# Rotary embedding of the first block on GpSimd, chunk by chunk, and one transpose group per weight tile

## The reference

```python
def diff_attention(h, w_qkv, w_o, lq1, lk1, lq2, lk2, subln_g, lam_init, cos, sin):
    qkv = h @ w_qkv                                    # 256x1024 @ 1024x3072
    q, k, v = jnp.split(qkv, 3, axis=-1)
    q = q.reshape(B_, S, A_N_HEADS, 2, A_HEAD_DIM)     # 8 heads, 2 halves of 64
    k = k.reshape(B_, S, A_N_HEADS, 2, A_HEAD_DIM)
    q = jnp.concatenate([apply_rope(q[..., :A_ROT], cos, sin), q[..., A_ROT:]], axis=-1)   # A_ROT = 16
    k = jnp.concatenate([apply_rope(k[..., :A_ROT], cos, sin), k[..., A_ROT:]], axis=-1)
    lam = (jnp.exp(jnp.sum(lq1 * lk1)) - jnp.exp(jnp.sum(lq2 * lk2)) + lam_init)
    ...                                                # softmax of q k^T, p0 - lam * p1, times v
```

## Time and profile before

| | us |
|---|---|
| median of 3 runs | 1056.72 |
| lowest, highest | 1055.93, 1057.69 |
| the profiled execution | 1057.23 |
| its span on the core | 1055.5 |
| its mean granted TensorE clock | 0.989 of full |

### The profile page before, as it was taken

The page is one execution under the profiler, slowest core; times in us unless marked ns, Lnnn a source line. Parts: engine busy times, 40 slices in busy tenths (PEclk is TensorE's granted clock), DMA queues, the critical chain, the costliest instruction groups (busy, mean ns, idle before and its releaser), DMA issues.

```text
span 1055.5 us, 12741 instructions
## 1 busy us (share of the span) xinstructions
PE 1001.1 (95%) x4744; PEld 820.3 (78%) x4744; DVE 735.9 (70%) x1030; ACT 543.0 (51%) x882; POOL 59.3 (6%) x100
## 2 busy tenths in 40 slices
PE   3899879999999999999999999999999999999997
PEld 2787567888888877777888887888889878888786
DVE  5989777977768787887765545737654676767753
ACT  3354654644434376665444435665555475555441
POOL 2100021000000410010000001100000010000000
PEclk9999889999999999999999999999999999999999
DMA  9999313998889845248875553856544357665551
GB/s 339 315 370 350 102 61 106 352 342 274 266 299 328 299 160 200 75 125 257 292 227 185 177 197 101 266 170 199 145 134 149 111 183 236 180 182 180 177 179 41
DMA packets 126966, 219.86 MB, mean 208 GB/s; under 512 B 9235, under 2 KB 78088, under 8 KB 126904
## 3 DMA queue, kind: packets, MB, share of 16 engines
q1 hardware_dynamic: 125488, 216.05, 62.3%
q0 software_dynamic: 1088, 2.87, 1.0%
q10 hardware_dynamic: 328, 0.12, 0.0%
HBM read 217.96 MB, written 1.05 MB: 207 GB/s over the span
## 4 chain that ended last, share of the span: by engine, by line
PE 80%; DVE 10%; ACT 4%; DMA 3%; issue 2%; POOL 0%; SPq 0%; DVEq 0%; POOLq 0%; ACTq 0%
PE bank L1815 15%; PE bank L1817 15%; PE bank L1816 15%; PE bank L1830 5%; PE bank L1831 5%; PE bank L1832 5%; DVE w_lo L1100 3%; PE bank L1877 2%; PE bank L1879 2%; PE bank L1878 2%; ACT w_hi L620 1%; DMA raw<-in_a_w_qkv 1%; PE bank L1933 1%; PE bank L1860 1%; PE bank L1909 1%
## 5 line engine op out<-in xcount | busy, mean ns | idle before, releaser
L1100 DVE TENSOR_TENSOR w_lo<-raw,w_hi 128x1024 fp32r<-128x1024 f32 x312 | 378.3, 1223 | 229.2 <-ACT w_hi L620 228.9
L620 ACT ACTIVATE w_hi<-raw 128x1024 fp32r<-128x1024 f32 x312 | 326.3, 1059 | 344.8 <-PE bank L1817 189.0
L1815 PE MATMUL bank<-w_hi,h_hi 128*128 128x512 f32 x768 | 307.4, 400 | 4.6 <-DVE h_lo L1281 2.7
L1817 PE MATMUL bank<-w_hi,h_lo 128*128 128x512 f32 x768 | 300.7, 392 | 0.0
L1816 PE MATMUL bank<-w_lo,h_hi 128*128 128x512 f32 x768 | 300.1, 391 | 0.0
L1815 PEld LDWEIGHTS bank<-w_hi,h_hi 128*128 128x128 f32 x768 | 145.0, 189 | 35.1 <-issue 4.0
L1817 PEld LDWEIGHTS bank<-w_hi,h_lo 128*128 128x128 f32 x768 | 144.8, 189 | 31.1
L1816 PEld LDWEIGHTS bank<-w_lo,h_hi 128*128 128x128 f32 x768 | 145.2, 189 | 29.7 <-issue 1.0
L1830 PE MATMUL bank<-w_hi,u_hi 128*128 128x512 f32 x200 | 78.6, 393 | 0.8 <-ACT av L1047 0.8
L1832 PE MATMUL bank<-w_hi,u_lo 128*128 128x512 f32 x200 | 77.9, 389 | 0.0
L1831 PE MATMUL bank<-w_lo,u_hi 128*128 128x512 f32 x200 | 77.9, 389 | 0.0
(11 more groups left out here) (317 smaller groups left out, 1258.8 us busy)
## 6 DMA issues: line engine op xcount, KB each, us to landing
raw<-in_f_w_in SPq DMA_DIRECT2D x176, 256.0 KB
ada<-in_ada_w SPq DMA_DIRECT2D x86, 512.0 KB, 5.8
raw<-in_w_in SPq DMA_DIRECT2D x46, 512.0 KB
raw<-in_f_w_out SPq DMA_DIRECT2D x44, 512.0 KB
raw<-in_w_up SPq DMA_DIRECT2D x88, 256.0 KB
raw<-in_a_w_qkv SPq DMA_DIRECT2D x24, 512.0 KB
raw<-in_w_down SPq DMA_DIRECT2D x22, 512.0 KB
raw<-in_b_w_qkv SPq DMA_DIRECT2D x12, 512.0 KB
```

The source lines that it names most:

```text
L620: nc.scalar.activation(w_hi[:, m % SPL], raw[:, m % RAW], ACT.Copy).then_inc(hi_done, 1)
L1100: ve.tensor_tensor(w_lo[:, m % SPL], raw[:, m % RAW], w_hi[:, m % SPL].bitcast(F32), ALU.subtract).then_inc(lo_done, 1)
L1815: mm(o, hi, w_hi[:, s, k], start=(u == 0 and k == 0), stop=False)
L1817: last = mm(o, lo, w_hi[:, s, k], start=False, stop=(u == 3 and k == 1))
```

## The change

Four edits, all in the first block:

1. The rotation leaves DVE. GpSimd does it chunk by chunk (chunks 0 to 3), each as soon as ACT has copied that chunk, with four instructions for a chunk: two products with the sine half of the table into `rope_t`, one product in place with the cosine half, one sum. Each covers both token tiles. A semaphore `rope_c` counts the chunks.
2. The transposes move from two groups before each of tiles 19 to 22 to one group before each of tiles 13 to 20, in the order 0 to 7. Group n waits for `rope_c` to reach n // 2 + 1; group 0 also waits for `evac` to reach 3. The copies to `qkT` follow on DVE (even groups) and ACT (odd groups).
3. Lambda on DVE is split: the two dot products at m = 7, the three small steps at m = 11.
4. The later waits on `rope_ok` count one less, since the first rotation no longer raises it.

```diff
-QK_STEPS_A = (19, 20, 21, 22)
-QK_ORDER_A = (0, 4, 1, 5, 2, 6, 3, 7)
+QK_STEPS_A = {13 + n: n for n in range(8)}
...
+            pool.wait_ge(side_in, 16 * SIDE)
+            for c in range(4):
+                pool.wait_ge(evac, c + 1)
+                q = proj[:, :, c * CH:(c + 1) * CH].rearrange("p t (h d) -> p t h d", d=64)[:, :, :, 0:16]
+                tmp = rope_t[:, :, 8 * c:8 * c + 8]
+                spread = lambda tab, n: tab.unsqueeze(2).to_broadcast([P, T, 8, n])
+                for h in range(2):
+                    last = nc.gpsimd.tensor_tensor(tmp[:, :, :, 8 * h:8 * h + 8], q[:, :, :, 8 - 8 * h:16 - 8 * h],
+                                                   spread(rope_a_sb[:, :, 1, 8 * h:8 * h + 8], 8), ALU.mult)
+                last.then_inc(rope_p, 1)
+                pool.wait_ge(rope_p, 2 * c + 1)
+                nc.gpsimd.tensor_tensor(q, q, spread(rope_a_sb[:, :, 0], 16), ALU.mult).then_inc(rope_p, 1)
+                pool.wait_ge(rope_p, 2 * c + 2)
+                nc.gpsimd.tensor_tensor(q, q, tmp, ALU.add).then_inc(rope_c, 1)
...
             for m in range(24):
-                if m in QK_STEPS_A:
-                    n = 2 * (m - QK_STEPS_A[0]) + 1
-                    f = QK_ORDER_A[n]
+                if m in QK_STEPS_A and QK_STEPS_A[m] % 2:
+                    n = QK_STEPS_A[m]
                     act.wait_ge(qk_t, n + 1)
...
+            def minus_lambda_end():
                 v_.wait_ge(setup, 4)
...
             for m in range(16):
+                if m in QK_STEPS_A and QK_STEPS_A[m] % 2 == 0:
+                    n = QK_STEPS_A[m]
+                    v_.wait_ge(qk_t, n + 1)
+                    ve.tensor_copy(qkT[:, 2 * n:2 * n + 2], bank[4 + n % 4][:].rearrange("p (k s) -> p k s", k=2)).then_inc(qk_d, 1)
                 low(QKV_A + SPL + m)
-                if m == 10:
+                if m == 7:
                     minus_lambda()
+                if m == 11:
+                    minus_lambda_end()
...
             for m in range(16, 24):
-                if m == 16:
-                    rotate(0, 32, rope_a_sb, rope_t, 4)
...
             for m in range(8, 24):
                 if m in QK_STEPS_A:
-                    pe.wait_ge(rope_ok, 1)
-                    for n in (2 * (m - QK_STEPS_A[0]), 2 * (m - QK_STEPS_A[0]) + 1):
-                        qk_transposes(n, QK_ORDER_A[n])
+                    n = QK_STEPS_A[m]
+                    if n == 0:
+                        pe.wait_ge(evac, 3)
+                    pe.wait_ge(rope_c, n // 2 + 1)
+                    qk_transposes(n, n)
```

More of the change, by code:

```diff
@@ L285, in program @@
         rope_ok = sem("rope_ok")
+        rope_p, rope_c = sem("rope_p"), sem("rope_c")
         qk_t = sem("qk_t")
@@ L767, in _ @@
             for m in range(24):
-                if m in QK_STEPS_A:
-                    n = 2 * (m - QK_STEPS_A[0]) + 1
-                    f = QK_ORDER_A[n]
+                if m in QK_STEPS_A and QK_STEPS_A[m] % 2:
+                    n = QK_STEPS_A[m]
                     act.wait_ge(qk_t, n + 1)
-                    nc.scalar.activation(qkT[:, 2 * f:2 * f + 2], bank[4 + n % 4][:].rearrange("p (k s) -> p k s", k=2),
+                    nc.scalar.activation(qkT[:, 2 * n:2 * n + 2], bank[4 + n % 4][:].rearrange("p (k s) -> p k s", k=2),
                                          ACT.Copy).then_inc(qk_a, 1)
@@ L1371, in _ @@
             for m in range(16, 24):
-                if m == 16:
-                    rotate(0, 32, rope_a_sb, rope_t, 4)
-                if m in QK_STEPS_A:
-                    n = 2 * (m - QK_STEPS_A[0])
-                    f = QK_ORDER_A[n]
+                if m in QK_STEPS_A and QK_STEPS_A[m] % 2 == 0:
+                    n = QK_STEPS_A[m]
                     v_.wait_ge(qk_t, n + 1)
-                    ve.tensor_copy(qkT[:, 2 * f:2 * f + 2], bank[4 + n % 4][:].rearrange("p (k s) -> p k s", k=2)).then_inc(qk_d, 1)
+                    ve.tensor_copy(qkT[:, 2 * n:2 * n + 2], bank[4 + n % 4][:].rearrange("p (k s) -> p k s", k=2)).then_inc(qk_d, 1)
                 low(QKV_A + SPL + m)
@@ L2097, in keys_b @@
             def keys_b():
-                pe.wait_ge(rope_ok, 2)
+                pe.wait_ge(rope_ok, 1)
                 pair_transposes_b(proj[:, :, 1024:1280], 4)
             def queries_b(p):
-                pe.wait_ge(rope_ok, 2 + p + 1)
+                pe.wait_ge(rope_ok, 1 + p + 1)
                 if p >= 2:
@@ L2275, in _ @@
                 if m == QK_STEPS[0]:
-                    pe.wait_ge(rope_ok, 7)
+                    pe.wait_ge(rope_ok, 6)
                     pe.wait_ge(gm_y, 1)
```

## The result

| | before | after |
|---|---|---|
| median, run in turn on one chip (19 runs each) | 1057.58 | 1059.24 |
| the same on a second chip (22 and 8 runs) | 1057.52 | 1059.70 |
| time of the profiled execution | 1057.23 | 1058.57 |
| its span | 1055.5 | 1056.8 |

The ratio of after to before is 1.0016 [1.0009, 1.0023] in the first series and 1.0023 [1.0013, 1.0032] in the second. So the change costs 1.7 us (1.0 to 2.4) and 2.4 us (1.4 to 3.4): slower than the forecast of +0.9, and around the border of 0.2% that was set between no change and slower. The absolute 1059.24 lies inside the range on record (1054.8 to 1060.0). Of its distance to the predicted 1057.6, 0.9 us is the kernel before itself, which ran at 1057.58 here and not at 1056.72.

The account below looks back on a forecast made before the run. PE, busy 95% of the span, was taken as the bound. Tiles 29.92, wait 3.38, transposes 3.59 and low clock 1.55 sum to 38.44 us against 37.55: +0.9, so 1057.6, range 1054.8 to 1060.0.

Parts of the forecast that it names:

- The rotation's wait goes, the one for chunk 2 comes: PE's 2.41 us loss before the old transposes goes; a 3.38 us wait for ACT's chunk 2 copy comes before tile 13.
- Lambda's split makes the wait shorter: Dot products at m = 7 spare ACT's exponential its wait for DVE, making PE's new wait 1.5 us shorter.
- The exponential right behind the table load: On ACT before the copy of chunk 2, the exponential starts 0.01 us after the table load ends.
- rival (d): On ACT, a longer wait behind the table load, making the kernel slower; chance 5%.
- The transposes cost the same in eight blocks: On PE, eight blocks of four cost 3.59 us against 3.63 for the old four blocks of eight.
- GpSimd is hidden, DVE's freed time is worth nothing: GpSimd's chunks take 2.7 to 7.9 us, hidden, counted as zero; PE is not short of `w_lo`, so DVE's time gains nothing.
- Rival (e): GpSimd is late beside busy DVE, costing once chunks exceed about 8.5 us; at 10 us +9, 1066; chance 5%.
- The low clock behind the new wait: PE's clock falls after idling 3.2 us before the first transposes, costing 1.55 us (0 to 3.2).
- Rival (b): The clock stays up behind PE's new wait: 1.55 us less, -0.7, 1056.0; chance 8%.
- Rival (a): Chunk 2 is free when PE asks: 4.0 us gained, 1052.7; half the way -2.3, 1054.4; together 9%.
- The low clock in tile 19: 4.40 - 2.72 - 0.09 = 1.59: In the kernel before, PE loses 1.59 us to low clock behind the rotation wait; counted as going with it.
- Rival (c): The clock pays twice, behind the new wait or in the attention: +2.5 us, 1059.2; chance 12%.

Follow-up runs that it names:

- lam10: The changed kernel with lambda's dot products back at m = 10 instead of m = 7; ratio to the kernel before 1.0058.
- dve15: Against steps15, the rotation of each chunk is done by DVE instead of GpSimd; ratio to the kernel before 0.9968.
- before_again: The kernel before, unedited, profiled a second time; start of tile 6 to end of tile 23 took 56.13 us, against 57.23 in its first profile.
- steps15: The changed kernel with the transpose groups before tiles 15 to 22 instead of 13 to 20; median 1054.4, ratio to the kernel before 0.9968.
- fill: The changed kernel with five unused matmuls of 128x512 in front of PE's wait for chunk 2; ratio to the kernel before 0.9998.

## Why the prediction was right in its mechanism and short in its size

The measured median of after lies in the range on record, and each link of the chain happened. The change itself came out at nearly twice the forecast or more, for one term in the main, the second to last below.

- **The rotation's wait goes, the one for chunk 2 comes.** Right. 3.02 us lost against 3.38 forecast, released by ACT's copy. It came out 0.36 shorter because PE was later relative to tile 16's transfer: tile 12's last matmul starts 0.35 after the split in after (71.58, 71.23), and 0.01 before it in before. In the other two profiles of after the idle time was 3.0, nearer to the forecast's 3.2. That the window of the first profile is 38.44 us, exactly the sum forecast, is partly luck: the wait is 0.36 too long in the sum, and the blocks of transposes and the low clock together are as much too short.
- **Lambda's split makes the wait shorter.** Right in kind; the credit of 1.5 us was too small: lam10 shows 3.6. It didn't enter the sum, because the sum took the split as done.
- **The exponential right behind the table load.** Right: 0.01 us (72.31 + 1.28 = 73.59, 73.60), now at the very place, and 0.01 or 0.02 in every other profile in which it didn't wait for DVE. So nothing but the load's 1.28 us itself stands there, and rival (d), a longer wait behind the load, falls. No run shows the case to which the forecast gave 5%, and half of that in the chance of slower.
- **The transposes cost the same in eight blocks.** Right. Tile 14 with its block takes 82.87 - 79.67 = 3.20 us against 2.72 + 0.44 = 3.16 forecast: 0.04 too little, 0.3 over the seven tiles behind later blocks.
- **GpSimd is hidden, DVE's freed time is worth nothing.** Right. Chunks took 4.4, 6.1, 5.1 and 3.6 us, inside the bounds of 2.7 and 7.9 though mostly far above the lower one. (In the lower one the 0.3 us for a chunk's waits was an estimate of mine; GpSimd's gaps between its instructions add up to 0.16 us in chunk 1 and in chunk 3. The upper bound would not quite have been hidden: four chunks of 7.9 us behind 62.2 end at 93.8, and the fourth was wanted at 93.5; so the price starts at 7.8 us a chunk and not at 8.5.) In after PE never waits for GpSimd, and dve15 shows the engine to be indifferent. Rival (e) falls.
- **The low clock behind the new wait.** Right: tile 13 lasts 4.43, 1.62 too long, against 1.55 forecast, and the clock fell in all three profiles. Rival (b) falls. One of the two cases that spoke against it, the first weight tile, was misread, though: there PE was slow before the idle time already (see the last section). Rival (a), chunk 2 free in time, happened in no profile of after. It needed the copy 3.2 us earlier, and the split of tile 16 stood 19.06, 19.21 and 19.22 us behind the start of tile 6 in the three, 19.42 in the profile before the prediction.
- **"The low clock in tile 19: 4.40 - 2.72 - 0.09 = 1.59", as a fixed term of before.** This is the mis-sized term. The 4.40 is the time of tile 19, 89.24 to 93.64, and the lower level was a granted clock of 0.50 there (89.37 to 92.37). It is there in one of four profiles. Where it is missing, the stretch is 1.13 us shorter (56.10 and not 57.23), since 0.46 is lost again, most of it by the wait for the copy to `qkT`, which the sum did not have. Over the four profiles before's stretch is 56.38 on the mean, 0.85 less than in the one profile, and the change costs 1.8 us by the profiles and not 0.9. The prediction took from the change a saving of 1.59 ("that term goes, and the 2.41 and 1.59 behind it with it") that before usually doesn't have to give. The single profile could not show this. It could have warned: in the same profile PE was idle for 1.97 us before tile 6 and its clock stayed at full (1.00 from 50.00 to 52.00), so idle time alone might not settle the outcome at 2.25.
- **Rival (c), 1059.2, has nearly the measured time, by a mechanism that did not happen.** It wanted a second low stretch in after, behind the new wait or in the attention. Behind the wait there is one, also behind 2.99, 3.02 and 6.56 us. The attention was not slower: 43.5, 44.5 and 44.7 us in after, 44.7, 44.4, 42.4 and 44.3 in before. The second "payment" was before's, missing. That the measured time comes near this rival is chance.

How often before's clock falls over many executions can't be said from four profiles. Nor is it known whether the chips differ in it, and so why the change cost 1.7 us on one chip and 2.4 on the other; the two intervals overlap (1.0 to 2.4, 1.4 to 3.4), so there may be nothing to explain.

## What to carry to other kernels

When work is moved earlier on the engine that is the bound, look up what its new place has to wait for before counting the old wait as won: here the inputs were early enough, but the PSUM bank was not, and two tiles (2 x 2.72 = 5.4 us) of delay turned +1.7 into -3.4 us. An idle time of PE is priced with the clock behind it, and where such a stretch stands in the profile before, take a second and a third profile before booking it as a saving. Test separately which of the parts pays: here the switch of engine, the larger edit, was worth nothing once the steps were right.

## What the runs showed of the hardware

- **The clock's reaction to idle time of PE is not the same in each execution.** In the projection the granted clock stayed at full behind 0.94, 1.62 and 1.96 or 1.97 us in every profile that has such a gap; behind 2.21 to 2.34 it fell in one of four; behind 2.86 to 6.56 in four of four. Over the 4.9 us from the first transposes the mean is 0.65 in before's first profile and in the three of after, 0.66 in lam10, and about 1.6 us are lost: transposes and tile together take 5.27 us in before's first profile against 3.69 in before_again, and 4.84 in each profile of after and 4.80 in lam10 against the 3.20 of tile 14 with its block.
- **PE ran at about half its pace in places where the granted clock reads 1.00** (0.43 us from one start to the next against 0.23). The prediction's second example of a fall, the first weight tile behind 2.68 us of idle time, is such a place. In before's profile its matmuls start 0.43 us apart, as in tile 19, but the row of the stretch has 1.00 where tile 19 has 0.65:

```profile
28.80 0.63 PE L1816 MATMUL bank<-w_lo,h_hi 128*128 128x512 f32 x1
29.22 0.63 PE L1817 MATMUL bank<-w_hi,h_lo 128*128 128x512 f32 x1
```

```profile
28.20:30.00 1.80, 1.79 (x4) 1.49 (x5) 1.80 (x3) 1.80 (x3) 0.00 (x0) 1.00 1.05 388
```

  And it is no fall behind the idle time of 2.68 us: PE was as slow before it. In the same profile eight transposes took 1.97 us, against 1.03 in the projection (at 93.64), and sixteen matmuls of one column 3.57 us, against 1.84 for the same shape in before_again. The clock column reads 1.00 for them too:

```profile
19.37 1.97 PE L1922 MATMUL bank<-ident,xn 128*128 128x128 f32 x8 [3.42 <-DVE xn L1146]
...
21.95 3.57 PE L1933 MATMUL bank<-ones,ada_acc 128*128 128x1 f32 x16
```

  The first tile began slow in every profile here and lasted 4.23 us in the one before the prediction, up to 5.29 in steps15. So the 1.51 that the prediction took from it is no price of an idle time. It is best to read the pace from the starts of the matmuls and the granted clock beside it.
- **DVE and GpSimd slowed each other, both ways.** Beside GpSimd's rotation in after DVE's `low` took 1.45 to 1.76 us and its folds 1.47 to 1.73, where without GpSimd they took 1.22 and 1.28 in dve15. One `low` of after was not slowed: at 88.34 us it took 1.22, and GpSimd's product beside it 1.77. GpSimd's products and sums of 256 elements took 1.58 to 1.77 beside DVE and 0.74 to 0.76 at best, one of these (67.76 us) beside the `low` that took 1.76. In steps15 this cost PE nothing, since its stretch is that of dve15; in lam10 it made PE's wait longer, through lambda.

DVE in order of time, after, while GpSimd works on chunk 1:

```profile
70.92 1.48 DVE L1114 TENSOR_TENSOR w_lo<-raw,w_hi 128x1024 fp32r<-128x1024 f32 x1
72.32 1.73 DVE L1144 SCALAR_TENSOR_TENSOR ada_u<-ada,cond,ada_u 128x1024 f32<-128x1024 f32 x1
```

DVE in dve15, without GpSimd:

```profile
71.96 1.22 DVE L1099 TENSOR_TENSOR w_lo<-raw,w_hi 128x1024 fp32r<-128x1024 f32 x1
73.09 1.28 DVE L1129 SCALAR_TENSOR_TENSOR ada_u<-ada,cond,ada_u 128x1024 f32<-128x1024 f32 x1
```

- **In fill a product of two float32 operands took PE 0.86 us for 512 columns**, in two records each and with a granted clock of 1.00 (70.78 to 75.07), against 0.23 for one of the three products of a weight tile, whose operands are in the reduced-precision type.
